# A mixture-of-experts tail: the residual rides with the first experts' rows, and three token tiles are read early

## The chip, the cores and the metric

The kernel runs on one core of one Trainium2 chip. The metric is device time in microseconds (us), the median of several executions. TensorE (PE) does the matmuls, VectorE (DVE) and ScalarE (ACT) the elementwise work, GpSimd (POOL) issues the indirect DMAs and does a few small operations, SyncE (SP) issues most of the other DMAs. All of them share the core's 16 DMA engines.

## The reference, cut to what matters

One decoder layer of 1024 tokens and width 1024. Attention comes first and is not touched. Then each token picks one of 4 expert groups and two of the group's 8 experts:

```python
x = x + gate_a * (o @ w_out)                       # residual after attention
h = rms_norm(x, g_moe) * (1 + scale_m) + shift_m
y = 0
for e in range(32):                                # gates are zero but for two experts per token
    hid = silu(h @ w_gate[e]) * (h @ w_up[e])      # 1024 -> 256
    y = y + gates[:, e:e+1] * (hid @ w_down[e])    # 256 -> 1024
x = x + gate_m * y
return rms_norm(x, g_final)
```

All arrays are float32. An expert's three matrices are 3 MB together, the 32 experts 96 MB.

## The kernel before, in words

Tokens are held as T = 8 tiles of 128 rows (XT). After the router, every (token, expert) pair is given a slot in a list of NSTEP = 20 steps of 128 slots; a step holds four pieces of 32 slots, each of one expert, the busiest experts first. What does not fit goes to an overflow list, whose loop runs only if a count that is read at run time is above zero; with these inputs it does not run.

The normed rows of all tokens lie in DRAM (h2_dram), and so does y_dram, which has 2 x 1024 rows: row t for a token's first expert and row 1024 + t for its second. The 20 steps are the expert phase:

- POOL gathers the 128 token rows of a step into SBUF (`gather`, L712). It gathers steps 0 to 3 first. Then, for each n, it issues gather(n + 4) and after it scatter(n). gather(n) waits for t_ps, that is for PE to have turned the rows of step n - 2 out of one of the two buffers xg.
- PE turns the rows (`turn_rows`, L2018), ACT and DVE scale them (`ev_t`, DVE L1545), PE multiplies with gate and up weights (`gate_up`, L2031), ACT and DVE make the hidden values (`ev_hid`, L1526 and L1528), PE turns these (L2040) and multiplies with the down weights (`down_proj`, L2054), one PSUM bank for each half of 512 columns.
- DVE multiplies each half by the modulation row out_row into one of two buffers ysb (`ev_y`, L1536), and POOL scatters the 128 rows to y_dram (`scatter`, L719).

PE's order in step n is: turn the hidden values of n, gate_up(n + 1), turn_rows(n + 2), down_proj(n). SP loads the weights into 7 + 7 places (`gate_up_load` L421, `down_load` L426): when the last step that uses a place is done on PE, SP loads the next expert there. The last loads follow the gate_up and the down_proj of step 15. After these SP reads the tokens' own rows back from h2_dram into XT (L592, tiles 0 to 5 after step 15 and the other two after step 17), since the weights had taken their place.

The tail: when all 20 scatters have landed, POOL raises rows_out (L764), and SP reads for every tile the two blocks of expert rows (L617, 16 DMAs of 512 KB). Tiles 0, 2, 4 and 6 are combined on PE (`add_into`, L2092): XT times the identity, plus each block times a diagonal of routing weights that ACT has written (L1014). Tiles 1, 3, 5 and 7 are combined on DVE by two operations (`combine`, L1579 and L1581). For each tile in the order 0 to 7 ACT takes the sum of squares (L1026), POOL makes the reciprocal root (L768, L769), DVE scales and multiplies by g_final (`finish`, L1591), and SP stores the tile (L620).

## Time and profile before

| | |
|---|---|
| median of 3 runs | 1008.46 us (1006.54 to 1008.69) |
| the profiled execution's own time | 1007.81 us |
| its span, first to last instruction | 1006.0 us |
| mean granted TensorE clock | 0.987 |
| PE busy | 953.2 us (95% of the span) |
| DVE busy | 594.4 us (59%) |
| ACT busy | 400.9 us (40%) |
| POOL busy | 119.5 us (12%) |
| bytes moved by DMA | 189.88 MB, mean 189 GB/s |

In the profile PE is TensorE's matmuls and PEld its weight loads, which overlap. A queue's engine name with a q (SPq, POOLq) is its sequencer. L712 is line 712 of the kernel before. DMA queue q1 carries what SP issues, q10 what ACT issues, q0 what POOL issues. A share of DMA of 1.00 means that all 16 DMA engines are busy. The span and the run's time differ by 1.8 us, which lies outside the instructions.

### The profile page before, as it was taken

How to read it: one execution, taken by the hardware profiler on the slowest of the kernel's cores; microseconds unless marked ns; L12 is line 12 of the kernel's file. 1: busy time of each engine (PE TensorE's matmuls, PEld its weight loads, DVE VectorE, ACT ScalarE, POOL GpSimd, SP SyncE). 2: the span in 40 equal slices, each digit the busy share in tenths (PEclk: the TensorE clock that was granted, in tenths of full speed). 3: DMA queues.
4: the chain of work that ended last, by engine and by line, in shares of the span. 5: the costliest groups of instructions: out<-in, count | busy, mean ns of one | idle time of the engine just before them, and what ended most of it. 6: DMA issues, size and time to landing. Idle time of an engine off the chain costs nothing.

```text
span 1006.0 us, 15057 instructions
## 1 busy us (share of the span) xinstructions
PE 953.2 (95%) x5352; PEld 520.0 (52%) x5352; DVE 594.4 (59%) x1597; ACT 400.9 (40%) x909; POOL 119.5 (12%) x219
## 2 busy tenths in 40 slices
PE   3899999999999999999999999999899999998984
PEld 2465576444447856677766555556533433333421
DVE  3388647999999799987777333456422222232217
ACT  6131135666660388877668221212211111121113
POOL 3001000000007510110000000000111111111004
PEclk9899999999999999999999999998999999998999
DMA  9997100110102000040000411089799999999979
GB/s 325 334 358 277 43 22 21 43 41 22 42 23 47 1 1 1 2 169 22 1 2 2 167 45 40 23 352 382 307 409 422 421 419 421 420 420 421 418 296 367
DMA packets 70381, 189.88 MB, mean 189 GB/s; under 512 B 10200, under 2 KB 37136, under 8 KB 58016
## 3 DMA queue, kind: packets, MB, share of 16 engines
q1 hardware_dynamic: 62176, 170.53, 44.2%
q0 software_dynamic: 5760, 16.78, 4.3%
q10 hardware_dynamic: 2368, 1.57, 0.6%
q8 instruction: 44, 0.72, 0.3%
q14 instruction: 33, 0.27, 0.1%
HBM read 174.17 MB, written 18.89 MB: 192 GB/s over the span
## 4 chain that ended last, share of the span: by engine, by line
PE 65%; DVE 20%; DMA 6%; issue 4%; SPq 2%; ACT 1%; POOL 1%; POOLq 0%; DVEq 0%; ACTq 0%
PE PS L2031 12%; PE PS L1908 11%; DVE BIAS L1168 8%; PE PS L2054 6%; PE PS L1801 6%; PE PS L1844 5%; PE PS L1866 4%; DMA X<-in_w_down_dram 3%; PE PS L1762 3%; PE PS L1714 3%; PE PS L1861 2%; DVE X L1232 2%; PE PS L1739 2%; PE PS L1679 2%; PE PS L2018 2%
## 5 line engine op out<-in xcount | busy, mean ns | idle before, releaser
L1714 PE MATMUL PS<-HT,X 128*128 128x512 f32 x384 | 168.8, 593 | 0.0
L1714 PEld LDWEIGHTS PS<-HT,X 128*128 128x128 f32 x384 | 72.5, 190 | 92.4 <-issue 92.4
L878 ACT ACTIVATE X<-X,nmx 128x128 f32<-128x128 f32 (+7 forms) x128 | 98.4, 770 | 51.5 <-DVE nmx L1232 51.0
L2031 PE MATMUL PS<-QKV,HT 128*32 128x512 f32 (+2 forms) x560 | 113.0, 594 | 2.4 <-ACT HT L976 1.7
L1908 PE MATMUL PS<-QKV,HT 128*128 128x512 f32 x256 | 113.7, 597 | 0.0
L1168 DVE TENSOR_SCALAR_CACHE_REDUCE BIAS<-SC,W 128x384 f32<-128x384 f32 (+3 forms) x128 | 96.4, 809 | 1.1
L1526 DVE TENSOR_TENSOR HT<-PS,HT 128x256 f32<-128x256 f32 x20 | 8.5, 425 | 140.9 <-ACT HT L984 140.9
L861 ACT ACTIVATE X<-SC,W 128x896 f32<-128x896 f32 x64 | 69.6, 1088 | 43.0 <-DVE W L1156 43.0
L1801 PE MATMUL PS<-QKV 64*128 64x512 f32 (+3 forms) x384 | 79.0, 517 | 1.6 <-DVE nmx L1232 1.1
L1908 PEld LDWEIGHTS PS<-QKV,HT 128*128 128x128 f32 x256 | 47.4, 190 | 53.7 <-issue 53.6
L1844 PE MATMUL PS<-ident,X 128*128 128x128 f32 x432 | 63.2, 279 | 2.1 <-DVE X L1250 2.0
L2054 PE MATMUL PS<-QKV,HT 128*32 128x512 f32 (+2 forms) x272 | 57.4, 630 | 4.3 <-DMA X<-in_w_down_dram 3.9
L984 ACT ACTIVATE HT<-PS 128x256 f32<-128x256 f32 x20 | 7.7, 384 | 131.8 <-PE PS L2031 131.8
L1232 DVE CUSTOM_DVE_ANT_0 X<-PS,R 128x128 f32<-128x128 f32 (+7 forms) x80 | 50.8, 673 | 14.6 <-PE PS L1801 8.6
L2031 PEld LDWEIGHTS PS<-QKV,HT 128*32 128x32 f32 (+2 forms) x560 | 32.3, 117 | 47.9 <-issue 44.2
L1844 PEld LDWEIGHTS PS<-ident,X 128*128 128x128 f32 x432 | 47.2, 141 | 11.3 <-issue 8.5
L1232 DVE CUSTOM_DVE_ANT_0 X<-PS,SC 128x1024 f32<-128x1024 f32 (+5 forms) x48 | 42.0, 887 | 17.9 <-PE PS L1801 17.8
L2031 PE MATMUL PS<-W,HT 128*32 128x512 f32 (+2 forms) x144 | 49.3, 593 | 0.0
L1536 DVE TENSOR_TENSOR HT<-PS,R 128x512 f32<-128x512 f32 x40 | 27.7, 692 | 35.0 <-PE PS L2054 34.9
L1801 PEld LDWEIGHTS PS<-QKV 64*128 64x128 f32 x384 | 31.6, 185 | 27.8 <-issue 20.4
L1060 DVE SCALAR_TENSOR_TENSOR QKV<-QKV,cact 128x512 f32<-128x512 f32 x56 | 42.1, 752 | 2.0
L1861 PEld LDWEIGHTS PS<-QKV,HT 128*128 128x128 f32 x288 | 34.5, 191 | 16.6 <-issue 9.2
(306 smaller groups left out, 1544.9 us busy)
## 6 DMA issues: line engine op xcount, KB each, us to landing
QKV<-in_w_down_dram SPq DMA_DIRECT2D x20, 1024.0 KB, 24.5
QKV<-in_w_gate_dram SPq DMA_DIRECT2D x19, 1024.0 KB, 17.3
QKV<-in_w_up_dram SPq DMA_DIRECT2D x19, 1024.0 KB, 20.4
QKV<-in_w_ada_dram SPq DMA_DIRECT2D x8, 2048.0 KB, 12.5
QKV<-in_w_ada_dram SPq DMA_DIRECT2D x8, 1024.0 KB, 12.4
X<-in_w_in_dram SPq DMA_DIRECT2D x16, 512.0 KB, 3.8
X<-in_w_down_dram SPq DMA_DIRECT2D x8, 1024.0 KB, 22.3
QKV<-expert_rows SPq DMA_DIRECT2D x16, 512.0 KB, 10.3
```

Of the source, the lines that this page charges most:

```text
L861: act.activation(RL[:, n % 2, 0:w], SC[:, sc_off[t]:sc_off[t] + w], ACT.Sign, bias=tk[:, 4, i:i + 1].bitcast(F32), scale=-1.0, accum_out=c ...
L878: act.activation(sc, sc, ACT.Exp, bias=nmx[:, i % 4, m:m + 1], scale=-1.0, accum_out=rs[:, i, m:m + 1]).then_inc(exp_done, 1)
L1060: link(dve.scalar_tensor_tensor(out=w[:, 0, :], in0=w[:, j, :], scalar=cact[:, j:j + 1], in1=w[:, 0, :], op0=ALU.mult, op1=ALU.add))
L1168: dve.tensor_scalar(BIAS[:, i % 3, 0:w], SC[:, sc_off[t]:sc_off[t] + w], thr.bitcast(F32)[:, i:i + 1], 0.0, ALU.is_lt, ALU.add, accum_out= ...
L1232: dve.tensor_tensor_reduce(sc_buf[i % 4][:, m, 0:w], PS[:, 2 * m:2 * m + 2, :].rearrange("p a n -> p (a n)")[:, BANK * n:BANK * n + w], aw ...
L1714: end = pe.matmul(PS[:, 2 * b + half, :], WS[:, b, j, :], HT[:, j, BANK * half:BANK * (half + 1)], start=(j == 0), stop=(j == KC - 1))
L1801: end = pe.matmul(PS[:, 2 * m + n + c0 // BANK, 0:c1 - c0], QKV[rows_m, q0:q0 + P], QKV[rows_m, k0 + c0:k0 + c1], start=True, stop=True)
L1844: end = pe.transpose(PS[:, 4 + g % 2, c0:c0 + P], sc_buf[i % 4][:, m, P * b:P * (b + 1)], ident[:, :])
L1861: end = pe.matmul(PS[:, 6 + h % 2, slot], turned_at(i)[:, g % 4, P * (b - b0):P * (b - b0 + 1)], vf[:, u * S + P * b:u * S + P * (b + 1)], ...
L1908: end = pe.matmul(PS[:, n % 4, :], HT[:, k, P * (n // 2):P * (n // 2 + 1)], wo[:, k, BANK * (n % 2):BANK * (n % 2 + 1)], start=(k == 0), s ...
L2031: end = pe.matmul(PS[at, 2 + b, :], hgT[b][:, P * c_ + at.start:P * c_ + at.stop], WGU[w][:, c_, :, :], start=(c_ == 0), stop=(c_ == KC - 1))
L2054: end = pe.matmul(PS[at, 5 + h, :], hidT[b][:, P * c_ + at.start:P * c_ + at.stop], WDN[w][:, c_, BANK * h:BANK * (h + 1)], start=(c_ == 0 ...
```

## The change

The residual no longer waits in SBUF or comes back from h2_dram at the end. The rows that POOL gathers for an expert are the tokens' own rows, so each step adds its result to them before the scatter: for a token's first expert the scattered row is own row + weight * out_row * y, for its second it is weight * out_row * y alone. A tile's result is then a plain sum of its two blocks.

- The rows stay in the buffers. xg and ysb give way to four buffers `held`; step n uses held[n % 4] for its gather, adds in place and scatters from there. So gather(n) for n >= 4 waits for y_out of step n - 4, that is for scatter(n - 4) to have landed, and POOL's order for each n is gather(n + 3), then scatter(n).
- `ev_y` has two dependent DVE operations for each half instead of one: PSUM = PSUM * weight * out_row, then held = held * is_first + PSUM. It no longer waits for y_out.
- The slots' weights and the flags for first experts are made ahead of step 0: `weigh_experts` moves ahead of `ev_t(0, 0)` and gets four more small operations, three operations of `spread_weights` lay the weights (each as three bfloat16 parts) out by slot, 16 bfloat16 matmuls of PE (`list_weights`, between turn_rows(0) and gate_up(0)) bring them into slot order, and DVE reduces them (`keep_weights`). SP's load of out_row and down_load(6) wait for those matmuls.
- The 8 reads back from h2_dram are gone, and so are ACT's 8 diagonals.
- Early in the kernel, ahead of the attention, two DMAs copy the first 3 tiles of x into the two halves of y_dram, so that every row holds some finite number; POOL waits for them ahead of scatter(0).
- Ahead of step LATE = 18 (when down_proj(17) is done on PE), SP waits for the scatters of steps 0 to 17 to land and reads tiles 0, 1 and 2 (6 DMAs of 512 KB). POOL waits for these reads to land before it issues scatter(18).
- After rows_out SP reads only tiles 3, 4, 5, 7, 6 (10 DMAs). POOL gathers into tiles 0, 1 and 2 those rows that steps 18, 19 and the overflow wrote (6 indirect DMAs, each of whose other indices are out of bounds and skipped). `late_rows` makes these indices on DVE during gate_up(0).
- Tiles 0, 1, 2 and 6 are summed on PE by the identity, tiles 3, 4, 5 and 7 on DVE by one addition each. The order of squares, roots and finishing is 3, 0, 4, 1, 5, 2, 7, 6.

```diff
             for n in range(NSTEP + 1):
...
-                    back = {last_use[25]: range(0, 6), last_use[26]: range(6, T)}
-                    if n - 1 in back:
-                        for t in back[n - 1]:
-                            sp.dma_start(XT[:, t, :], h2_dram[P * t:P * (t + 1), :]).then_inc(x2_back, 16)
+                    if n == LATE:
+                        for b in range(2):
+                            sp.wait_ge(y_out[b], 16 * (LATE // 2))
+                        for t in range(AHEAD):
+                            expert_rows(t, yg_ahead)
...
             def gather(n):
 
-                if n >= 2:
+                if n >= 4:
+                    pool.wait_ge(y_out[n % 2], 16 * (n // 2 - 1))
+                elif n >= 2:
                     pool.wait_ge(t_ps, n - 1)
-                pool.indirect_dma_start(out=xg[n % 2], out_offset=None, in_=h2_dram,
+                pool.indirect_dma_start(out=held[n % 4], out_offset=None, in_=h2_dram,
...
             pool.wait_ge(route_done, 2)
+            pool.wait_ge(yg_ahead, 32)
             for n in range(NSTEP):
-                if n + 4 < NSTEP:
-                    gather(n + 4)
+                if n >= 1 and n + 3 < NSTEP:
+                    gather(n + 3)
+                if n == LATE:
+                    pool.wait_ge(yg_ahead, 32 + 32 * AHEAD)
                 scatter(n)
...
             pool.sem_inc(rows_out, 1)
-            for t in range(T):
+            pool.wait_ge(route_done, 3)
+            for t in range(AHEAD):
+                for k in range(2):
+                    pool.indirect_dma_start(out=yg[t][k], out_offset=None, in_=y_dram,
+                                            in_offset=bass.IndirectOffsetOnAxis(
+                                                ap=late_row[:, EARLY * k + t:EARLY * k + t + 1], axis=0),
+                                            bounds_check=2 * S - 1, oob_is_err=False).then_inc(yg_late[t], 16)
+            for i, t in enumerate(last):
...
-            def ev_y(e, b, stored):
-
-                dve.wait_ge(y_out[b], stored * 16)
+            def ev_y(e, buf, weight, is_first, counted):
+
                 for h in range(2):
                     part = slice(BANK * h, BANK * (h + 1))
                     dve.wait_ge(dn_ps, 2 * e + h + 1)
-                    dve.tensor_tensor(ysb[b][:, part], PS[:, 5 + h, :], out_row[:, part], ALU.mult).then_inc(y_sb, 1)
+                    dve.scalar_tensor_tensor(out=PS[:, 5 + h, :], in0=PS[:, 5 + h, :], scalar=weight, in1=out_row[:, part],
+                                             op0=ALU.mult, op1=ALU.mult).then_inc(hh_done, 1)
+                    dve.wait_ge(hh_done, counted + h + 1)
+                    dve.scalar_tensor_tensor(out=held[buf][:, part], in0=held[buf][:, part], scalar=is_first,
+                                             in1=PS[:, 5 + h, :], op0=ALU.mult, op1=ALU.add).then_inc(y_sb, 1)
...
             dve.wait_ge(modc_set, 1)
+            weigh_experts()
+            link(dve.tensor_scalar(row_first[:, 0:NSTEP], PS[:, 2, NSTEP:2 * NSTEP], float(S) + 0.5, None, ALU.is_lt))
+            spread_weights(low_tok, NSTEP, weight_is)
             ev_t(0, 0)
-            weigh_experts()
...
-            pe.wait_ge(x2_back, 16 * T)
             for i, t in enumerate(mixed):
-                if i == 2:
-                    pe.wait_ge(rows_out, 1)
-                add_into(i, ident[:, :], XT[:, t, :], True, False)
-            pe.wait_ge(diag_done, 8)
-            for i, t in enumerate(mixed):
-                pe.wait_ge(yg_in[t], 32)
-                add_into(i, diag[:, i, 0, :], yg[t][0], False, False)
-                add_into(i, diag[:, i, 1, :], yg[t][1], False, True).then_inc(mix_ps, 1)
+                pe.wait_ge(yg_late[t] if t < AHEAD else yg_in[read.index(t)], 32)
+                add_into(i, ident[:, :], yg[t][0], True, False)
+                add_into(i, ident[:, :], yg[t][1], False, True).then_inc(mix_ps, 1)
```

## Rows read from the trace of the kernel before

**Rows 1.** The page: busy time of PE, and DMA's share in 40 slices.

```profile
PE 953.2 (95%) x5352; PEld 520.0 (52%) x5352; DVE 594.4 (59%) x1597; ACT 400.9 (40%) x909; POOL 119.5 (12%) x219
...
DMA  9997100110102000040000411089799999999979
```

**Rows 2.** Busy time in a stretch of five steps; last: clock, DMA share, GB/s.

```profile
800.00:860.00 60.00, 60.00 (x364) 23.23 (x362) 17.54 (x40) 11.38 (x30) 10.12 (x10) 1.00 1.02 421
```

**Rows 3.** The chain of waits in order of time: start us, length us, what.

```profile
737.29 3.57 PE PS L2054 x32
...
753.40 7.00 PE PS L2031 x64
760.41 1.09 PE PS L2018 x8
...
765.50 7.00 PE PS L2031 x64
...
785.36 3.57 PE PS L2054 x32
...
807.80 1.09 PE PS L2018 x8
...
889.43 30.68 DMA X<-in_w_down_dram
...
967.28 3.31 DMA expert_rows<-HT,SC
```

**Rows 4.** PE in order of time at its one wait for a weight.

```profile
920.36 1.08 PE L2054 MATMUL PS<-QKV,HT 128*32 128x512 f32 x3 [3.86 <-DMA X<-in_w_down_dram]
```

**Rows 5.** SP's issues in order of time: first issue us, length of the group.

```profile
929.14 22.35 SPq L592 DMA_DIRECT2D X<-h_rows  x8
970.65 9.62 SPq L617 DMA_DIRECT2D QKV<-expert_rows  x16
```

**Rows 6.** The tail in order of time: start us, length us, engine, line.

```profile
975.69 3.67 PE L2092 MATMUL PS<-QKV,SC 128*128 128x512 f32 x8 [1.31 <-DMA QKV<-expert_rows]
...
982.40 3.70 PE L2092 MATMUL PS<-QKV,SC 128*128 128x512 f32 x8 [3.04 <-DMA QKV<-expert_rows]
...
996.36 1.02 ACT L1026 ACTIVATE HT<-PS 128x1024 f32<-128x1024 f32 x1 [2.20 <-PE PS L2092]
...
1001.70 1.28 DVE L1591 SCALAR_TENSOR_TENSOR X<-X,ss,BIAS 128x1024 f32<-128x1024 f32 x1 [0.39 <-POOL ss L769]
```

**Rows 7.** DVE at the start of the expert phase; in brackets its idle time before.

```profile
717.72 1.36 DVE L1545 TENSOR_SCALAR HT<-PS,gm,modc 128x128 f32<-128x128 f32 x4 [5.62 <-PE PS L2018]
...
720.89 0.17 DVE L1492 TENSOR_SCALAR eps_row<-eps_row 128x8 f32<-128x8 f32 x1
```

**Rows 8.** The page: DVE's output operation of all steps, mean ns of one.

```profile
L1536 DVE TENSOR_TENSOR HT<-PS,R 128x512 f32<-128x512 f32 x40 | 27.7, 692 | 35.0 <-PE PS L2054 34.9
```

**Rows 9.** POOL's instructions in order of time: start us, length us, idle before.

```profile
742.44 1.02 POOL L719 DMA_INDIRECT expert_rows<-HT,SC  x1 [3.02 <-DVE HT L1536]
750.18 1.03 POOL L712 DMA_INDIRECT HT<-h_rows,SC  x1 [6.72 <-PE PS L2018]
754.53 1.01 POOL L719 DMA_INDIRECT expert_rows<-HT,SC  x1 [3.32 <-DVE HT L1536]
...
951.89 0.98 POOL L719 DMA_INDIRECT expert_rows<-HT,SC  x1 [10.21 <-DVE HT L1536]
```

**Rows 10.** Queue 0's packets, MB, DMA share, in 754:758.5 and in 758.5:763.

```profile
q0 software_dynamic: 144, 0.52, 28.5%
...
q0 software_dynamic: 144, 0.37, 20.8%
```

**Rows 11.** The view of line 712, all 20 gathers: issue to landing.

```profile
DMA to landing us min/median/max: 5.0/8.8/10.0
```

**Rows 12.** Line 421, weight loads issued at 727.1 and at 832.4: issue to landing.

```profile
DMA to landing us min/median/max: 6.0/6.0/6.0
...
DMA to landing us min/median/max: 12.7/12.7/12.7
```

More of the change, by code:

```diff
@@ L613, in _ @@
             sp.wait_ge(rows_out, 1)
-            for t in range(T):
-                for k in range(2):
-                    row = S * k + P * t
-                    sp.dma_start(yg[t][k], y_dram[row:row + P, :]).then_inc(yg_in[t], 16)
-            for t in range(T):
-                sp.wait_ge(fin_done, t + 1)
+            for i, t in enumerate(read):
+                expert_rows(t, yg_in[i])
+            for i, t in enumerate(last):
+                sp.wait_ge(fin_done, i + 1)
                 sp.dma_start(out[0, P * t:P * (t + 1), :], XT[:, t, :]).then_inc(fin_out, 16)
@@ L755, in _ @@
                 pool.wait_ge(ov_list, 2)
+                for b in range(2):
+                    pool.wait_ge(y_out[b], 16 * uses(b))
                 with pool.Fori(0, NOV // 2) as i:
@@ L1011, in _ @@
             act.dma_start(gfin, g_final.partition_broadcast(P)).then_inc(act_in, 16)
-            for i, t in enumerate(mixed):
-                for k in range(2):
-                    act.activation(diag[:, i, k, :], ident[:, :], ACT.Copy, scale=rt[:, 5 + k, t:t + 1]
-                                   ).then_inc(diag_done, 1)
-            for t in range(T):
+            for n, t in enumerate(last):
                 if t in mixed:
@@ L2061, in weights_of, with list_weights @@
                         sorted({(w % places, 16 * (w // places + 1)) for w, _, _ in parts[n]}))
-            turn_rows(0, 0, 16)
+            def list_weights(bank, at, tiles, rows, weights):
+                for q in range(T):
+                    for k in range(2):
+                        end = pe.matmul(PS[:, bank, at:at + 3 * tiles], rows[:, k, q, :],
+                                        weights[:, k, q, :, :].rearrange("p a n -> p (a n)"),
+                                        start=(q == 0 and k == 0), stop=(q == T - 1 and k == 1))
+                return end
+            turn_rows(0, 0, 16, 0)
+            pe.wait_ge(weights_at, 3)
+            list_weights(6, 0, NSTEP, row_is, weight_is).then_inc(sel_ps, 1)
             gate_up(0, 0, *weights_of(0, GUS))
-            turn_rows(1, 1, 16)
+            turn_rows(1, 1, 16, 1)
             for n in range(NSTEP):
```

159 lines of the change are left out of this document (106 added, 53 removed).

## The prediction

> **What bounds the kernel now.** I read the page first, then the chain of waits over the last 350 us, then the busy times by stretch, and last POOL's own timeline with the packets of its queue. PE is busy for 95% of the span [rows 1], and DMA's row of slices is empty in the middle and full from about 650 us on [rows 1]. In the expert phase both are full: PE 60.00 us of 60, and DMA at a share of 1.02 with 421 GB/s [rows 2]. The chain of waits runs on PE, one step in 12.1 us (gate_up starts at 753.40 and at 765.50), up to a down weight that was issued at 889.43 and lands 30.68 us later, at 920.1 [rows 3]; PE has then waited for it for 3.86 us [rows 4]. What the reader is to see: a step that becomes longer ahead of 916 us is free up to those 3.9 us in all, and dear beyond them. After the last step comes a tail: the last scatter takes 3.31 us [rows 3], reads start at 970.65 [rows 5], the last tile is finished at 1001.70 + 1.28 = 1002.98 [rows 6], and its store ends at 1006.0.
>
> **The start of the phase.** DVE is idle for 5.6 us ahead of 717.7, while the first gather is under way [rows 7]. The 10 moved operations, four new ones, one flag and the three larger ones go there: 15 small ones at 0.2 us (the 10 stood between 719.1 and 721.1 [rows 7]) are 3.0 us, three of 320 elements at no more than the 0.69 us of a 512-element one [rows 8] are 2.1 us. They end some 0.5 us ahead of 717.7. PE's 16 small matmuls lie beside ACT's and DVE's scaling of the first rows, 1.36 us on DVE [rows 7]. Cost 0; if the cover fails, 1 us at most. The load of out_row is first used 20 us later. The copies of x into y_dram lie where DMA's slices are at 0 or 1 tenths [rows 1]: 0.
>
> **DVE and ACT in the steps.** A half's output takes two dependent operations instead of one. I price the second like the first, 0.69 us [rows 8], and with the wait between them 0.75 us. DVE has 17.5 us of work in 60 [rows 2], so 3 us more per step do not make it the bound. What counts is that scatter(n) can be issued 0.75 us later. The bank is free again well before the next down_proj.
>
> **The gathers: the term that decides.** Before, gather(n + 4) waited only for PE's turning of step n + 2. Now it waits for scatter(n) to land, as its buffer is the one that is scattered. The chain from the end of down_proj(n) to landed rows of step n + 4, piece by piece:
> - down_proj(0) ends at 737.29 + 3.57 = 740.86 [rows 3], its scatter is issued at 742.44 [rows 9]: 1.58, now with 0.75 more 2.33 us.
> - Scatter issued to landed. No row gives it, as nobody waited for it visibly. Scatter(1) is issued at 754.53 [rows 9]; queue 0 moves 144 packets in 754:758.5, which are those of the gather issued at 750.18 (at the median it lands at 759.0), and 144 more in 758.5:763, which are the scatter's [rows 10]. So it takes up to 8.4 us; the bounds are 3.31, the last scatter with DMA nearly idle [rows 3], and 10.0, the slowest gather [rows 11]. I take 8.1, near to the row of the same operation under the same load.
> - The landing to POOL's next issue: 0.8 us, as from the end of turn_rows(3) at 749.4 to 750.18 [rows 9].
> - The gather: 8.8 us, bounds 5.0 and 10.0 [rows 11].
>
> The sum is 20.0 us. PE wants the rows at 760.41 [rows 3], 19.55 us after 740.86; for step 4 the distance is 807.80 - 788.93 = 18.9 [rows 3]. With a mean of 19.3 the chain is 0.7 us too long, and as it spans two of PE's steps, that alone lengthens a step by 0.35 us.
>
> But there is a second loop. Gather and scatter share queue 0. The gather's 144 packets and the scatter's 144 stand one behind the other and do not mix [rows 10], so I read it as one queue in order, though in this case the scatter came just late enough not to wait. Then the new order is: scatter(n) lands, 0.8, gather(n + 4) takes 8.8, and only behind it go the packets of scatter(n + 1), which need another 3.7 us (758.5 to 763 is 4.5 at the most, and a step's scatter moves 0.37 MB against 0.52 of that gather [rows 10]). One round of the loop is 0.8 + 8.8 + 3.7 = 13.3 us, against 12.1 for PE's step: 1.2 us more per step, as soon as scatter(n + 1) waits behind gather(n + 4), which is so from step 1 (the gather comes at 743.19 + 8.1 + 0.8 = 752.1 and lands at 760.9, the scatter at 755.3 would have its packets move from 759.3).
>
> The Trainium skill (DMA: Bandwidth & Descriptors, Queues, rings and completion order) says that each DMA engine takes the descriptors of one ring in order and switches between rings by the packet. By that rule gathers and scatters queue up as in my second loop, and the weights of SP's queue are interleaved with both.
>
> How many steps are stretched? Steps 4 to 19 give 15 intervals. The weights' backlog is what stretches the latencies, and it is least near 832 us: a load takes 12.7 us there against 6.0 when the queue had just begun to fill [rows 12], so it holds 6.7 us of work. PE's lateness of 1.2 us per step uses that up after some six steps; then DMA has gaps, gather and scatter fall towards 5.0 and 3.3 us, the loop is 12 us or less and nothing is added for about four steps. That leaves 11 intervals: 11 x 1.2 = 13.2, and the first stall 0.6 (760.9 + 0.1 against 760.41), in sum 13.8 us. Of that 3.9 us disappear in the wait at 916 us [rows 4], as the weights' arrival is set by DMA, which stays busy: **+9.9 us** at the last down_proj. Its ends: 0 (the latencies of a quieter queue) and 15 x 1.5 + 0.6 - 3.9 = 19.
>
> **The tail.** The 8 reads back (from 929.14 on, 4 MB [rows 5]) came after the last weights, so dropping them makes no weight earlier; they only leave DMA idle for the early reads. Scatter(17) is landed some 4 us after its issue with DMA quiet. Then SP reads 3 tiles. Before, with as empty a queue, tile 2 was there at 982.40 - 970.65 = 11.7 us after the first issue [rows 5, 6]. Scatter(18) waits for this: from scatter(17)'s issue 4 + 0.4 + 11.7 + 0.8, then 1.3 for the next issue and 3.3 for scatter(19) to land, 21.5 us. Before, from its issue at 951.89 [rows 9] to 970.65, it was 18.8; with DVE's 0.75 the reads of the tail start **3.5 us later** relative to PE (ends 1 and 6).
>
> After that start, called R, POOL's first two gathers of the late rows are issued at R + 0.7 and R + 2.0, and land by R + 7 to R + 9 (5.0 to 8.8 us, few rows); PE's four sums of 3.7 us each [rows 6] run from about R + 7.5 to R + 22.3, and tile 6 is there by R + 18. The last sum ends at 996.3; the tile's square, root and finishing are over by 1001.7, when the next is finished [rows 6]: 5.4 us, say 5.0; then 3.0 for the store (1002.98 to 1006.0). End at R + 30.3, against 1006.0 - 970.65 = 35.35 before [rows 5, 6]: **-5.0 us** (ends -8 if DVE and POOL keep closer, -2 if stores and reads collide). Late next is then PE's row of four sums.
>
> **Sum**, against the profiled execution's 1007.81: + 0 (start) + 9.9 (gathers) + 3.5 (scatter(18) held back) - 5.0 (fewer reads in the tail) = +8.4, so 1016.2. The profiled execution lies 0.65 below the median of 1008.46, within the runs' own spread of 2.2; I do not correct for it and say 1016.
>
> **The rivals.**
> - *A, the forecast:* queue 0 is in order and the loop of 13.3 us rules. For it: two kinds of row, [rows 11] and [rows 10], and the saturated DMA of [rows 2]. Against it: the scatter's 8.1 is inferred. 1016, own range 1011 to 1023. Chance 0.5.
> - *B, no queueing between gather and scatter, only the 20.0 us against 19.3:* 15 x 0.35 = 5.3, less 3.9 hidden, +1.4; with the tail's -1.5, no change: 1007.7. Chance 0.17.
> - *C, the other side: the chain fits in.* One mechanism: gather plus scatter under load take 0.7 us less than I say, 16.2 instead of 16.9, and the queueing stays below the slack; from 19.3 us down PE never waits. For it: some gathers land in 8.1 us, and DVE's 0.75 may be partly hidden. Then only the tail counts: +3.5 - 5.0 = -1.5, and with the better ends of both (+1, -5) down to -4: 1003.8 to 1006.3, likeliest 1005.5. Chance 0.17.
> - *D, the early reads give nothing:* A's steps, and scatter(18) is held for the full 6 us while the tail keeps its length but for 2: +9.9 + 6 - 2 = 1021.7. Chance 0.09.
> - *E, the loop never finds a quiet stretch:* 19 - 1.5 = +17.5 and more, 1025 to 1030. Chance 0.07.
>
> The Trainium skill has a rule by which C would win outright (the same page, Anatomy of one DMA): an indirect or other DMA of POOL takes about 2.0 us plus its bytes over 436 GB/s, an estimate of 3.0 us for 0.42 MB. The sum would be 2.33 + 3.0 + 0.8 + 3.0 = 9 us, far below 19, and the time 1006.3. The trace agrees only where DMA is quiet (3.31 us for the last scatter) and not in the steps (8.8 us), so this adds nothing to C's chance.
>
> **How the numbers follow.** About 0.2%, 2 us, is what a measurement can tell from no change. Slower: A, D and E, 0.66, less the part of A's low end that is below +2 (0.04): 0.62. Faster: most of C, 0.14. The same: B and the rest, 0.24. The range leaves out E's upper part and C's lowest part: 1005 to 1024.
>
> **What would show it.** In the profile of the changed kernel, waits of PE at turn_rows for the gather: some 14 us in about ten waits, steps of 13.3 us, and the wait for a down weight near 916 us gone or small. Scatters' packets that begin more than 4.0 us after their issue. SP's wait ahead of the early reads 4 to 5 us, POOL's wait ahead of scatter(18) some 8 us. The tail from SP's first late read to the end about 30 us. The forecast is wrong if PE never waits for a gather: then it is C.

## The result, and the profile after

| | before | after |
|---|---|---|
| median of the runs made side by side | 1008.23 us (4) | 1020.23 us (4; 1018.30 to 1022.01) |
| ratio, 95% interval | 1 | 1.0122, 1.0099 to 1.0145 |
| profiled execution | 1007.81 us | 1018.3 us |
| span of that execution | 1006.0 us | 1016.5 us |

The change makes the kernel slower by 12.0 us, and by 10.5 us between the two profiled executions, which is the difference that the views below account for. (The profiled execution of after is the fastest of its four.) The forecast was +8.4, in the range.

The page of after, against [rows 1] of before: PE's busy time and DMA's slices.

```profile
PE 946.7 (93%) x5352; PEld 518.8 (51%) x5352; DVE 626.0 (62%) x1645; ACT 398.1 (39%) x901; POOL 122.6 (12%) x225
...
PEclk9999999999999999999999999997999999999978
DMA  9997101011015000040000411299899989999577
```

DVE has 32 us more, nearly all of it the second operation of 40 halves at 0.75 us. PE has 6.5 us less work in a span that is 10.5 us longer, so it waits more. The row of clocks hides what matters below: the falls of the clock in the steps are too short for a slice of 25 us.

Busy times by stretch of after, columns as in [rows 2]; last are the granted clock, DMA's share and GB/s.

```profile
740.00:780.00 40.00, 37.35 (x316) 13.25 (x309) 15.61 (x31) 6.81 (x18) 6.22 (x7) 1.00 1.01 420
780.00:820.00 40.00, 36.33 (x166) 15.51 (x168) 15.69 (x30) 6.81 (x18) 6.67 (x7) 1.00 1.01 415
820.00:860.00 40.00, 37.96 (x237) 14.23 (x230) 15.50 (x30) 6.81 (x18) 6.21 (x7) 0.96 0.90 366
900.00:940.00 40.00, 37.13 (x248) 13.98 (x248) 15.67 (x30) 6.81 (x18) 6.07 (x6) 1.00 1.01 420
```

PE was busy for all of 800:860 before. Now it lacks 2 to 4 us of every 40. DMA stays full except in 820:860, where its share falls to 0.90: the quiet spell that the forecast speaks of. It is short: the share is 0.34 in 820:825, 0.80 in 825:830 and 1.01 from there on.

The waits of after: engine, line, what was waited for; us in total, times, the longest. L739 is the gather, L746 the scatter, L2093 PE's turning of the gathered rows, L2180 PE's sums of the tail, L617 SP's wait ahead of the early reads.

```profile
POOL HT L739 <- DMA expert_rows<-HT,SC: 133.2, 15, 10.2
...
PE PS L2180 <- DMA QKV<-expert_rows,SC: 17.9, 1, 17.9
...
PE PS L2093 <- DMA HT<-h_rows,SC: 15.1, 11, 2.2
...
POOL expert_rows L746 <- DMA SC<-expert_rows: 13.3, 1, 13.3
```

POOL now waits for a scatter to land before each of its 16 gathers from gather(4) on (one of these waits, of 10.4 us, the view puts down to "issue"), and PE waits 11 times, 15.1 us in all, for gathered rows. Before it waited for none of more than 0.4 us in sum. The wait for a down weight [rows 4] is gone.

The chain of waits of after, in order of time, against [rows 3]: start us, length us, what.

```profile
741.22 10.06 DMA expert_rows<-HT,SC
...
752.06 8.09 DMA HT<-h_rows,SC
...
760.19 1.16 PE PS L2093 x8
761.35 3.62 PE PS L2129 x32
...
764.99 0.77 DVE PS L1596
...
765.78 0.76 DVE HT L1599
...
767.33 9.06 DMA expert_rows<-HT,SC
...
777.15 9.29 DMA HT<-h_rows,SC
...
786.48 1.16 PE PS L2093 x8
```

Before, this chain ran on PE alone. Now it goes round: scatter, gather, turn, down_proj, DVE's two operations, scatter, and one round takes 786.48 - 760.19 = 26.3 us for two of PE's steps.

The same round in POOL's own order, against [rows 9].

```profile
752.06 1.03 POOL L739 DMA_INDIRECT HT<-h_rows,SC  x1 [9.81 <-DMA expert_rows<-HT,SC]
753.39 1.02 POOL L746 DMA_INDIRECT expert_rows<-HT,SC  x1 [0.30 <-issue]
764.21 1.01 POOL L739 DMA_INDIRECT HT<-h_rows,SC  x1 [9.80 <-DMA expert_rows<-HT,SC]
```

Scatter(1) is issued at 753.39, 1.3 us behind a gather, and has landed 0.8 us before 764.21: 10.0 us, where I had priced 8.1.

### The profile page after: what moved, and what is told of

It reads as the page before. It is cut to its first block, busy times and chain, and to the rows that moved or that the text cites. A ratio compares the mean times of both kernels' runs of the same rounds, so it can differ in the third digit from the quotient of the medians.

```text
span 1016.5 us, 15086 instructions
## 1 busy us (share of the span) xinstructions
PE 946.7 (93%) x5352; PEld 518.8 (51%) x5352; DVE 626.0 (62%) x1645; ACT 398.1 (39%) x901; POOL 122.6 (12%) x225
## 4 chain that ended last, share of the span: by engine, by line
PE 55%; DVE 20%; DMA 16%; issue 6%; ACT 1%; POOL 1%; SPq 0%; POOLq 0%; DVEq 0%; ACTq 0%
PE PS L1983 11%; DVE BIAS L1205 8%; DMA expert_rows<-HT,SC 7%; DMA HT<-h_rows,SC 6%; PE PS L1876 6%; PE PS L1919 5%; PE PS L2129 4%; PE PS L1941 4%; PE PS L2106 3%; PE PS L1837 3%; PE PS L1789 3%; PE PS L1936 2%; DVE X L1269 2%; PE PS L1814 2%; PE PS L2180 2%
## 5 line engine op out<-in xcount | busy, mean ns | idle before, releaser
L1919 PEld LDWEIGHTS PS<-ident,X 128*128 128x128 f32 x432 | 47.2, 141 | 11.4 <-issue 8.7
L1269 DVE CUSTOM_DVE_ANT_0 X<-PS,SC 128x1024 f32<-128x1024 f32 (+5 forms) x48 | 42.0, 887 | 17.9 <-PE PS L1876 17.8
L1876 PEld LDWEIGHTS PS<-QKV 64*128 64x128 f32 x384 | 31.6, 185 | 27.8 <-issue 20.4
L1017 ACT ACTIVATE HT<-PS,modc,gm 128x128 f32<-128x128 f32 x80 | 30.1, 455 | 36.4 <-PE PS L2093 36.4
## 6 DMA issues: line engine op xcount, KB each, us to landing
QKV<-in_w_ada_dram SPq DMA_DIRECT2D x8, 2048.0 KB, 15.6
```

The source lines that it names most:

```text
L1269: dve.tensor_tensor_reduce(sc_buf[i % 4][:, m, 0:w], PS[:, 2 * m:2 * m + 2, :].rearrange("p a n -> p (a n)")[:, BANK * n:BANK * n + w], aw ...
L1876: end = pe.matmul(PS[:, 2 * m + n + c0 // BANK, 0:c1 - c0], QKV[rows_m, q0:q0 + P], QKV[rows_m, k0 + c0:k0 + c1], start=True, stop=True)
L1919: end = pe.transpose(PS[:, 4 + g % 2, c0:c0 + P], sc_buf[i % 4][:, m, P * b:P * (b + 1)], ident[:, :])
```

## Where the 10.5 us went

POOL's issue times cut each profile into stretches that can be compared. G0 is the first gather's issue, S0, S17 and S19 those of scatters 0, 17 and 19, end is the end of the span. All times in us; the last column is what PE waited for on gathers and weights from G0 to S17. Waits for gathers of 0.3 to 0.7 us lie ahead of S0.

| kernel | G0 to S0 | S0 to S17 | S17 to S19 | S19 to end | PE's waits |
|---|---|---|---|---|---|
| before | 31.35 | 209.45 | 15.39 | 38.72 | gathers 0.4, a down weight 3.9 |
| after | 31.87 | 221.88 | 15.62 | 37.78 | gathers 15.1 in 11 |
| e1_wait_alone | 31.96 | 219.42 | 15.37 | 39.76 | gathers 15.7 in 15 |
| e2_light_weights | 31.87 | 214.56 | 17.07 | 37.11 | gathers 10.2 in 6 |
| e3_five_buffers | 32.26 | 213.95 | 16.38 | 36.93 | gathers 10.5 in 10 |
| e4_own_result_buffer | 32.68 | 207.96 | 22.37 | 36.45 | gathers 0.5, a weight 2.4 |
| e5_second_op_alone | 32.22 | 207.50 | 15.40 | 39.10 | gathers 0.5, a weight 3.3 |
| e6_late_rows_behind | 31.88 | 209.33 | 16.02 | 39.52 | a weight 3.7 |
| e7_two_ahead | 32.03 | 206.86 | 14.05 | 39.28 | a weight 3.2 |
| e8_quiet_weights | 32.82 | 202.32 | 16.92 | 36.78 | gathers 0.7 |
| e9_clock_kept | 32.13 | 208.67 | 13.85 | 46.19 | a weight 3.1 |
| e10_sums_sooner | 32.58 | 208.54 | 14.06 | 42.15 | gathers 0.5, a weight 2.8 |
| e11_clock_kept_short | 32.64 | 205.84 | 14.85 | 35.27 | gathers 0.5, a weight 1.9 |
| e12_plan_alone | 32.38 | 207.70 | 13.85 | 36.34 | gathers 0.3, a weight 2.1 |

Of after less before: +0.5 up to S0, **+12.4 in the steps**, +0.2 and -0.9 in the tail, and -1.7 ahead of G0 (709.35 against 711.09; in the executions of all these kernels it lies between 708.4 and 712.1 without order, so it is not the change's). The sum is 10.5.

The steps need one more look, at the one wait of before. The chain of before has the weight wait, and down_proj behind it:

```profile
920.11 0.25 issue
920.36 6.47 PE PS L2054 x32
```

and the stretches of before around it, columns as above (the last but two is the granted clock):

```profile
916.00:918.00 2.00, 0.50 (x5) 0.30 (x3) 1.91 (x6) 1.49 (x5) 0.73 (x1) 1.00 1.01 422
918.00:920.00 2.00, 0.00 (x0) 0.00 (x0) 0.22 (x1) 0.04 (x1) 0.28 (x1) 0.82 1.01 426
920.00:922.00 2.00, 1.64 (x8) 0.46 (x12) 0.00 (x0) 0.00 (x0) 0.00 (x0) 0.50 1.01 418
922.00:924.00 2.00, 2.00 (x16) 0.67 (x12) 0.00 (x0) 0.00 (x0) 0.00 (x0) 0.50 1.00 410
...
926.00:928.00 2.00, 2.00 (x18) 0.60 (x14) 0.69 (x1) 0.38 (x1) 0.00 (x0) 0.97 0.98 406
```

While PE stands still for 3.86 us its granted clock falls to 0.50, the 1.2 GHz level, and stays there for some 6 us of the work behind: this down_proj takes 6.47 us where others take 3.57 [rows 3]. So the wait cost 3.86 + 2.90 = 6.8 us, not 3.9, and before's 17 steps without it are 202.7 us, 11.9 each. After's are 221.88 / 17 = 13.05 each: 19.2 us added by the round, and 6.8 taken off with the weight wait that it hides.

The same happens once more in after. Two of its eleven waits, of 2.04 and 2.18 us, are followed by a lower clock; the chain of after at the first:

```profile
850.41 1.85 PE PS L2093 x8
852.26 4.54 PE PS L2129 x16
```

and the stretches there:

```profile
848.00:850.00 2.00, 0.37 (x4) 0.00 (x0) 0.85 (x2) 0.38 (x1) 0.00 (x0) 1.00 1.03 416
850.00:852.00 2.00, 1.59 (x8) 1.45 (x8) 0.00 (x0) 0.00 (x0) 0.00 (x0) 0.67 0.99 412
852.00:854.00 2.00, 2.00 (x8) 0.58 (x8) 1.37 (x4) 1.50 (x4) 0.00 (x0) 0.50 1.04 438
```

Turning and down_proj take 6.39 us where they take 1.16 + 3.62 = 4.78 in the other steps: 1.6 us more, and 1.3 at the second (1.97 + 4.14). The two steps are the longest of after, 15.8 and 15.7 us from scatter to scatter. With them the 19.2 us are 15.1 of waits, 2.9 of clock and 1.2 left over (behind a wait, turning takes 1.16 in place of 1.09 us). A wait of 2.24 us at 760.19 left the clock at 1.00, and so did one of 3.15 us for the same down weight in e7 below, so the length of the wait alone does not decide it.

## The experiments

The theory after the result: the scatter that must land before a gather is issued makes a round of DMA latencies, and these are long because weights fill DMA. Rivals: DVE's second operation costs the time; the order in queue 0 does, and not the chain through PE; the early reads and the tail do.

**e1: the wait alone.** The kernel before, with nothing but the gather's wait and its place in POOL's order.

```diff
             def gather(n):
+                if n >= 4:
+                    pool.wait_ge(y_out[n % 2], 16 * (n // 2 - 1))
...
-                if n + 4 < NSTEP:
-                    gather(n + 4)
+                if n >= 1 and n + 3 < NSTEP:
+                    gather(n + 3)
```

> The kernel before with one part of the change alone: gather(n + 4) also waits for scatter(n) to have landed (nothing else needs it here), and POOL issues gather(n + 3) ahead of scatter(n). One DVE operation for each half, residual and tail as before. Loop theory (PE waits for gathers that wait for landed scatters while DMA is saturated): slower than before, by one of two sizes. If only the chain down_proj, scatter, gather, turn_rows counts: 1.6 + 9.0 + 0.7 + 9.3 = 20.6 us against 19.3, over two steps, 0.6 us per step, 15 steps, less the 3.9 us hidden at the weight: +5, about 1013 us. If also the order in queue 0 counts (scatter behind gather, a round of 13.1 us): 1.0 us per step, +11, about 1019 us. Rival (the second DVE operation, the extra work at the start or the tail made it slower): within 1 us of before, 1008.

Measured: 1018.98 us against 1006.61, 1.0131 (1.0100 to 1.0163). The chain of waits of e1 (L2020 turns the rows, L2056 is down_proj):

```profile
795.19 9.48 DMA expert_rows<-HT,SC
...
805.49 8.47 DMA HT<-h_rows,SC
...
814.00 1.16 PE PS L2020 x8
```

The wait, with its place in POOL's order, is the whole loss. The kernel has no second operation on DVE, no early read, the old tail, and is as slow as the changed kernel; its steps take 219.4 us, 2.5 less than after's, and the clock does not fall in them (1.00 in all five stretches of 40 us), which is 2.9 of after's. The time is that of the larger of the two sizes expected, the one with the order in queue 0 in it; what that order adds here is read in the account of the prediction below.

**e5: DVE's second operation alone.** The kernel before, with two dependent operations for a half (the second adds 0.0 times a row, so that the result is the same).

```diff
-                    dve.tensor_tensor(ysb[b][:, part], PS[:, 5 + h, :], out_row[:, part], ALU.mult).then_inc(y_sb, 1)
+                    dve.tensor_tensor(PS[:, 5 + h, :], PS[:, 5 + h, :], out_row[:, part], ALU.mult).then_inc(hh_done, 1)
+                    dve.wait_ge(hh_done, counted + h + 1)
+                    dve.scalar_tensor_tensor(out=ysb[b][:, part], in0=out_row[:, part], scalar=0.0, in1=PS[:, 5 + h, :],
+                                             op0=ALU.mult, op1=ALU.add).then_inc(y_sb, 1)
```

> The kernel before with one other part of the change alone: DVE makes each half of a step's result in two dependent operations (the second adds the PSUM half to a row times zero). Gathers as before. Loop theory: nothing waits for DVE here, the last scatter is issued 0.8 us later; 0 to +1 us against before. Rival (the second operation stretches the steps): +0.9 us per step, up to +12 us.

Measured: 1006.79 against 1006.09, 0.9996 (0.9979 to 1.0014): no change. The later scatter costs nothing as long as nobody waits for it to land.

**e8: light weights.** The changed kernel, with the later weight loads cut to 256 of 2048 columns.

```diff
-                        gate_up_load(sp, expert_of(w), w % GUS)
+                        gate_up_load(sp, expert_of(w), w % GUS, n=256)
...
-                        down_load(sp, expert_of(w), w % DNS)
+                        down_load(sp, expert_of(w), w % DNS, n=256)
```

> The changed kernel, with all instructions of PE, DVE, ACT and POOL, but the weight loads from place 7 on bring only 256 of 2048 columns each (a part of the computation left out), as the loads of half size had left DMA busy at 0.8 to 0.9. Loop theory: DMA's share in the steps below 0.5, scatters and gathers land in 5 to 6 us, no wait of PE for a gather, steps of 12.1 us: from the first to the eighteenth scatter 206 to 208 us instead of 222, about 1002 to 1005 us in all. Rival (second DVE operation, PSUM written back by DVE): steps stay at 13 us.

Measured: 1000.09 against 1006.09, 0.9932 (0.9908 to 0.9957), 2 us under what was expected, as the landings and the steps are shorter than I had said. A stretch of e8, and the landing of its 20 scatters and 20 gathers:

```profile
740.00:780.00 40.00, 40.00 (x328) 14.37 (x321) 16.34 (x32) 7.02 (x19) 7.12 (x7) 1.00 0.40 129
```

```profile
DMA to landing us min/median/max: 2.9/3.4/4.3
...
DMA to landing us min/median/max: 3.6/4.3/10.2
```

and the same two views of after:

```profile
DMA to landing us min/median/max: 3.3/9.2/10.4
...
DMA to landing us min/median/max: 4.4/8.7/10.4
```

With DMA's share at 0.27 to 0.40 in the stretches of the steps a scatter lands in 3.4 us in place of 9.2 and a gather in 4.3 in place of 8.7, and PE waits for none in the steps. The wait is the same, the two transfers of the round are 10 us shorter together. That is what ties the loss to the weights' traffic and not to the wait as such. S0 to S17 is 202.32 us, which is what before's steps take without their weight wait (202.7): the 6.8 us priced above, from another side.

The Trainium skill (DMA: Bandwidth & Descriptors, Latency and other measured facts) puts the access of HBM at 0.2 us on average and 2 us at high load. The trace agrees in the direction only; the difference between e8 and after is 4.4 us for a gather and 5.8 for a scatter.

The traces' packet records show where it lies. A packet of 4 KB of queue 0 takes 0.159 us in e8 and in after alike (median of 740 to 940 us), so the packets do not become slower. They begin later and stand further apart. In after the first packet of scatter(0) comes 4.1 us after its issue, at 745.34, though queue 0 had sent nothing before it; in e8 it is 1.6 us. From a scatter's first to its last packet it is 3.3 to 5.3 us in after's steps under full DMA, and 1.0 to 2.3 us in e8, where the weights' packets are about as many but take 0.046 us each in place of 0.309. Ahead of that first packet DMA moves weights alone; behind gather(4)'s issue at 752.06, the view of queues in 752.5:756 has no queue but SP's:

```profile
q1 hardware_dynamic: 198, 1.47, 99.9%
```

What holds the first packet back for 2.5 us more than in e8, no run here shows.

**e2: half the gate and up weights.** The same as e8 with 1024 of 2048 columns and full down weights.

> The changed kernel, but from expert place 7 on each gate and each up load brings only half of its columns (0.5 MB instead of 1 MB); the other half of the place keeps old values, so that part of the computation is left out. PE, DVE, ACT and POOL do the same instructions. Loop theory: with DMA at about 0.7 of its share, scatters land in some 5 us and gathers in some 6 us, the chain is 14 us against 19.3, PE waits for no gather, and the wait for a down weight is gone too: 12.5 and some us less than the changed kernel, about 1004 to 1007 us, steps of 12.1 us. Rival (DVE's second operation or an extra PE instruction stretches the steps): steps stay at 13 us, 1016 us or more.

Measured: 1014.41 against 1006.61, 1.0090 (1.0053 to 1.0127). A miss: I had expected 1004 to 1007. The stretch 860:900 of e2 shows why:

```profile
860.00:900.00 40.00, 35.80 (x256) 13.70 (x258) 15.58 (x30) 6.57 (x18) 6.10 (x6) 0.96 0.93 324
```

DMA moved 324 GB/s, a quarter less, and was still busy for 0.93 of the time. The down weights, gathers and scatters were as large as ever, and of the halved rows' packets (4 KB in place of 8) half took no more than 0.159 us, against 0.309 for a full one, but their mean in this stretch was 0.197. So this run did not take the load away, and e8 had to.

**e3: a fifth buffer.** The changed kernel, with the gather waiting for the scatter of a step earlier, into one buffer more; for each n POOL issues gather(n + 4), then scatter(n), and g_final is loaded after the last scatter.

```diff
-        held = [HF[:, a:a + 1024] for a in (0, 1024, 4096, 5120)]
+        held = [BIAS[:, 2, :]] + [HF[:, a:a + 1024] for a in (0, 1024, 4096, 5120)]
...
-                if n >= 4:
-                    pool.wait_ge(y_out[n % 2], 16 * (n // 2 - 1))
+                if n >= 5:
+                    pool.wait_ge(y_out[(n - 5) % 2], 16 * ((n - 5) // 2 + 1))
```

> The changed kernel with a fifth row buffer (in the third kilobyte row of BIAS; g_final, which comes to lie there, is loaded after the last scatter): gather(n + 4) waits for scatter(n - 1) instead of scatter(n), everything else the same. Loop theory: PE gets 12 us more slack per gather, its waits for gathers are gone or small, steps of 12.1 us, total about 1008 us (start 0, tail -0 to -2 against before). If the order in queue 0 makes a loop of its own (round of 13.1 us), POOL falls behind PE by some 1 us per step: scatters issued to landed and gathers drift later through the phase, and the last few gathers may make PE wait a few us, 1008 to 1012. Rival (DVE's second operation, start, tail): 1018 or more, as the changed kernel.

Measured: 1012.04 against 1006.61, 1.0061 (1.0044 to 1.0078). Half of the loss is back, and what is left is the other round of the forecast. POOL's order in e3:

```profile
767.30 1.02 POOL L739 DMA_INDIRECT HT<-h_rows,SC  x1 [11.47 <-DMA expert_rows<-HT,SC]
768.62 1.02 POOL L746 DMA_INDIRECT expert_rows<-HT,SC  x1 [0.30 <-issue]
781.33 1.02 POOL L739 DMA_INDIRECT HT<-h_rows,SC  x1 [11.68 <-DMA expert_rows<-HT,SC]
782.65 1.01 POOL L746 DMA_INDIRECT expert_rows<-HT,SC  x1 [0.30 <-issue]
```

A gather, 1.3 us later a scatter that has long been ready, and 11.9 us later it has landed, which lets the next gather go. The chain of waits of e3 runs from scatter to scatter, with PE in none of its pieces:

```profile
782.65 10.63 DMA expert_rows<-HT,SC
...
795.42 11.22 DMA expert_rows<-HT,SC
```

Six of these in a row take 10.4 to 11.9 us, 11.2 on average, 2 us more than the 9.1 of the scatters in after's chain. The steps from scatter to scatter are 12.5 to 14.0 us, 13.3 on average, up to the sixteenth. This is the forecast's round through queue 0, at its size of 13.3 us. The packet records agree: the packets of these scatters begin 6.0 to 6.9 us after their issue (scatters 1 to 14), when the gather's are through, and not 4.1 to 4.3 us after it as with the queue free.

**e4: an own buffer for the result.** DVE writes the output to a buffer of its own, so the gather needs only DVE, and no landed scatter. POOL issues scatter(n) first and gather(n + 4) behind it, and DVE's output of a step waits for the scatter of the step before to have landed.

```diff
-                if n >= 4:
-                    pool.wait_ge(y_out[n % 2], 16 * (n // 2 - 1))
+                if n >= 4:
+                    pool.wait_ge(y_sb, 2 * (n - 4) + 2)
...
-                    dve.scalar_tensor_tensor(out=held[buf][:, part], in0=held[buf][:, part], scalar=is_first,
+                    dve.scalar_tensor_tensor(out=ysb[:, part], in0=held[buf][:, part], scalar=is_first,
```

> The changed kernel, but DVE writes the step's result into a buffer of its own (the same kilobyte row of BIAS) and POOL scatters from there. gather(n + 4) then waits only for DVE to have read the rows of step n, no longer for a scatter to land; POOL issues scatter(n), then gather(n + 4); DVE's result of step n + 1 waits for scatter(n) to have landed. Loop theory: the chain is 2.4 + 1.3 + 9 to 11 = 13 to 15 us against 19.3, PE waits for no gather, 12.1 us per step, about 1007 to 1009 us. No drift, as no gather hangs on a landed scatter. Rival (second DVE operation or tail): 1018 or more.

Measured: 1010.99 against 1006.61, 1.0041 (1.0020 to 1.0061), 2 us over what was expected. The steps are back to 207.96 us, with 0.5 us of waits for gathers. But S17 to S19 went from 15.6 to 22.4 us: the one result buffer makes step 19's output wait for scatter(18), which itself waits for the early reads.

**e6 and e7: that wait removed, and the tail in another order.** In e6 step 19 writes in place, and the tiles with late rows are summed last; e7 is e6 with two tiles read early in place of three, and the order of the tail's tiles fitted to that.

```diff
-                in_=ysb, in_offset=None,
+                in_=held[n % 4] if n == NSTEP - 1 else ysb, in_offset=None,
...
-        AHEAD = 3
-        read = (3, 4, 5, 7, 6)
+        AHEAD = 2
+        read = (2, 3, 4, 6, 5, 7)
```

> The kernel with a result buffer of its own, with two edits. Step 19 adds in place and is scattered from its row buffer, so it no longer waits for scatter(18). In the tail PE sums tile 3, which is read directly, first and then 0, 1, 2; DVE sums 4, 5, 7, 6; squares and finishing go in the order 3, 4, 5, 0, 7, 6, 1, 2. Loop theory with the tail as the late gathers' and PE's sums set it: the last scatter 5 us earlier than with the result buffer alone, the last sum of PE ends some 22 us after the tail's first read instead of 26: 6 to 9 us less than that kernel, 2 to 4 us less than before. If the tail is bound by the bytes it moves, only the 5 us of the scatter are won, and the time is that of before.

> The same with only two tiles read early instead of three: the early reads take some 4 us less, so that scatter(18) is no longer held by them for long, and one more tile (1 MB, 2.6 us) is read after the last scatter. If the hold counts, the last scatter is issued 1 to 1.5 us earlier and the whole is within 1.5 us of the kernel with three; if the tail's bytes count, it is 1 to 2.5 us slower.

Measured: e6 1008.12 and e7 1005.40 against 1006.09, 1.0016 (0.9999 to 1.0032) and 0.9990 (0.9977 to 1.0004). Both are level with before. The result buffer's wait is gone (S17 to S19 is 16.0 and 14.1 us), but both are misses: e6 was to be 2 to 4 us under before, and e7 within 1.5 us of e6 or slower, where its median is 2.7 us lower. With the round gone the early reads bring nothing that can be measured in these. PE has nothing to do between its last down_proj and the first rows of the tail, and the first sum then takes 6.56 us (e6) and 5.30 us (e7) in place of 3.7 [rows 6]; whether that is what the time goes by, the next four test.

**e9 to e12: PE kept at work, and DVE's order.** e9 is e7 with 48 multiplies into an unused bank ahead of the sums; e10 the same with the tiles' sums and finishing steps on DVE in another order; e11 is e10 with 26 multiplies; e12 is e10 without any.

```diff
+            for _ in range(48):
+                pe.matmul(PS[:, 7, 0:2 * P], ident[:, :], HT[:, KC - 1, BANK:BANK + 2 * P], start=True, stop=True)
             for i, t in enumerate(mixed):
```

```diff
             combine(3)
-            finish(2)
             combine(4)
+            finish(2)
...
             finish(0)
+            combine(7)
             finish(6)
             finish(1)
-            combine(7)
             finish(7)
```

> The kernel with a result buffer of its own and two tiles read early, plus 48 matmuls of 256 columns on PE between the last down_proj and the first sum of the tail, into a PSUM bank that nobody reads; they fill the 12 us in which PE was idle and the granted clock fell to 0.50, so that the first sum took 5.3 us. If that clock is on the chain: the first sum takes 3.7 us and the whole is 1 to 2 us less. If DVE's order of work or the bytes bound the tail: no change, within 0.5 us.

> The same with the 48 matmuls, and DVE adds tile 4 ahead of finishing tile 2, and tile 7 ahead of finishing 6 and 1 (before, it added tile 7 some 5 us after its rows had landed, and the last two tiles waited for that). If DVE's order is the tail's bound: 3 to 5 us less than with two tiles early alone, about 1001 us, 4 to 6 us less than before. If the tail is bound by the bytes of reads and stores: at most 1 us less.

> e10_sums_sooner with 26 idle multiplies in place of 48. In e10 they took 20.99 us for 96 records (0.437 us a call) and held the first sum back to 9.6 us behind the landing of its rows; 26 take 11.4 us, which ends them at about 973.8 us where e7_two_ahead's rows landed at 973.7. If the clock is what lengthened e7's first sum: the sum is at 3.5 to 3.7 us (5.3 in e7), the granted clock in 966:974 is near 1.00, and from the end of the first sum to the end it is 18.9 us as in e10 (22.5 in e7): span near 997, median 1000 to 1002, 0.7% under before. If the tail goes by the arrival of the last rows, it is within 1 us of e12.

> e7_two_ahead with only VectorE's order of sums and finishing steps in the tail changed, and no idle multiplies. If VectorE's order is what e10 gained over e9 (18.9 against 22.5 us behind the first sum), this is 1 to 3.5 us under e7_two_ahead: 1002 to 1004.4. If the last rows' landing is what ends the tail, it is e7's time (1005.4). The first sum stays at 5.3 us, at the fallen clock; e11 less this run is what the clock is worth, 1.6 us or less.

Measured: e9 1011.24 and e10 1009.45 against 1007.01, 1.0043 (1.0026 to 1.0061) and 1.0021 (1.0008 to 1.0034); e11 1003.03 and e12 1002.04 against 1005.55, 0.9975 (0.9958 to 0.9993) and 0.9964 (0.9945 to 0.9982). e9 and e10 miss because of their own size: the 48 multiplies took 20.99 us, two records a call, and held up the first sum. e11 has the size right. PE's sums and the multiplies ahead of them in e11, in order of time:

```profile
963.43 13.18 PE L2199 MATMUL PS<-HT,ident 128*128 128x256 f32 x52 [2.18 <-issue]
976.45 3.60 PE L2194 MATMUL PS<-SC,ident 128*128 128x512 f32 x8
```

and the first sum in e12, without multiplies:

```profile
976.60 5.78 PE L2194 MATMUL PS<-SC,ident 128*128 128x512 f32 x8 [13.82 <-DMA SC<-expert_rows]
```

The clock had fallen in e11 too (0.76 in 962:966, 0.81 in 966:970), but with the multiplies it is back at 1.00 in 970:974, where it is 0.50 in e12, and the first sum is 2.2 us shorter with it. So work on PE does bring the clock back and keep it. It does not pay, though: e11 is 1.0 us above e12 in the median, with intervals that overlap. In e11 the rows of a tile that DVE needs land only at 982.05 (its chain of waits), and PE's gain ends in a wait for them. DVE's order probably pays: e12 less its kernel before is -3.5 us, where e7's is -0.7, and e10 less e9, the same two orders with the multiplies, is -1.8 us; in both pairs the intervals just overlap. Against the forecast of 1002 to 1004.4 it is right, and e11's 1000 to 1002 is missed by 1.0.

**The version to keep** of all these is e12: 0.9964 of before, -3.5 us. It is the changed kernel with the result in a buffer of its own (so that no gather waits for a landed scatter), two tiles early, and DVE's order of e10. The gain is small, 0.18 to 0.55%.

## Why the prediction was right, and where its sizes were off

- *The start: 0.* G0 to S0 is 31.87 against 31.35, of which DVE's second operation is 0.75 by the forecast. Right.
- *DVE's second operation: +0.75.* From the end of down_proj(17) at 960.73 to scatter(17) at 963.10 is 2.37 us, forecast 2.33, and 1.55 before. Right, and e5 shows that it is free by itself.
- *The chain, 20.0 us.* The seven rounds in the chain of waits of after have 2.4 us from the end of down_proj to the scatter's issue (forecast 2.33), a scatter of 9.1 (8.50 to 10.06; forecast 8.1), 0.8 (0.8) and a gather of 9.2 (8.09 to 9.67; forecast 8.8): 21.5 us. The scatter is what I mis-sized. I had taken its price from one row of queue 0 whose packets ended by 763 [rows 10].
- *Which round rules: the step that failed.* The forecast let the queue's round (13.3) rule and gave the chain 0.35 us a step. The chain of waits of after runs through the chain: (21.5 + 4.8) / 2 = 13.1 us a step, with 4.8 for turning and down_proj. Its seven rounds cover 14 of the 17 steps; the other three go at PE's own pace (11.4 to 12.5 us from down_proj to down_proj), and with the two falls of the clock the mean is 13.05. It is B's chain with a scatter 1 us longer and a gather 0.4 us longer than priced, and it comes out at nearly A's size. Queueing behind a gather isn't needed for that: scatter(0), issued after POOL had sent nothing for 14 us, is the slowest of the chain with 10.06 us.
- *A's queue is real all the same.* By the packet records (queue 0 moves 144 packets for a gather or a scatter; I count them off in order of time) a scatter's packets in after begin 4.1 to 4.3 us after its issue where DMA is full and the gather was issued 3.5 us or more ahead of it. Where under the same load it was issued 1.3 to 3.1 us ahead, they begin 4.7 to 6.0 us after it, which is always 7.4 to 8.2 us after the gather's issue, so behind the gather's packets. In after this hardly touches the chain: its four scatters that stood behind a gather took 9.0 us on average, its three others 9.3. In e1, where DVE has one operation and the scatter follows the gather by some 2 us in most steps, the scatters of the chain took 10.2 us, and that uses up what the shorter DVE work saves. In e3, where the fifth buffer gives the chain room, A's round rules alone, with its 13.3 us. So for the changed kernel a forecast with only the chain in it and the right latencies would have been as good, and A's number was right in part by luck.
- *A sign that could not tell.* "Packets that begin more than 4.0 us after their issue" was to show the queue. In the trace of before, where every gather was issued 3.8 us or more ahead of the scatter, the scatters' packets already begin 4.1 to 4.5 us after their issue.
- *The steps, +9.9.* Measured +12.4. The term of 11 intervals at 1.2 and 0.6 (13.8) was 19.2: 17 intervals at 1.13. The quiet spell came close to where it was said (820:830, with a share of 0.34 at first; the forecast named 832 as the weakest point), but it was short: gather(9) and scatter(6) were quick (6.1 and 4.8 us), and PE went two steps without a wait, where four had been forecast; PE's waits were 15.1 us in 11, forecast 14 in about ten. Left out were the falls of the clock, 2.9. The hidden weight wait was 6.8 and not 3.9, as its length on PE is not its cost. The two errors, +5.4 and -2.9, took part of each other away.
- *Scatter(18) held back, +3.5.* From S17 to SP's first late read, R = 983.47, it is 20.4 us against 18.8, so +1.6. The hold itself costs nearly nothing. down_proj(19) ends at 976.09, its scatter could be issued 2.4 us later at 978.5, and it was issued at 978.72. Scatter(18), ready at about 974.1 (971.75 + 2.4), waited until 977.45, but scatter(19) was what the late reads needed. The early reads had landed at 976.68, 10.1 us behind SP's first issue (forecast 11.7). What did cost is the last scatter, 4.69 us in place of 3.31 [rows 3], right behind scatter(18).
- *The tail from R, 30.3.* It is 1016.5 - 983.47 = 33.0, against 35.35 before: -2.3 and not -5.0. The chain of waits of after shows the piece that failed:

```profile
978.72 4.69 DMA expert_rows<-HT,SC
...
985.64 8.27 DMA QKV<-expert_rows,SC
...
993.95 15.74 PE PS L2180 x32
1009.72 1.02 ACT HT L1063
```

  PE's first sum began at R + 10.5 and not at R + 7.5. The gather of the late rows was priced for few rows; it shared DMA with ten reads of SP (share 0.97 to 1.03 in 986:994) and took 8.3 us. Then the sums took 15.7 for 14.8 us at a clock of 0.50 at first, after PE had stood for 17.9 us. The rest was 6.8 for 8.0.
- *The sum.* In the forecast's terms 0 + 9.9 + 3.5 - 5.0; measured 0.5 + 12.4 + 1.6 - 2.3 and -1.7 ahead of G0, which is 10.5. Each sign was right, the largest term was a fifth too small.
- *The rivals.* B's chain came true and its size did not; its premise that nothing queues did not hold in e1 and e3, nor for after's scatters off the chain. C, the other side, needed gather and scatter to take 16.2 us or less; they took 18.3. The Trainium skill's rule by which C would have won (DMA: Bandwidth & Descriptors, Anatomy of one DMA) gives some 6 us for the two, an estimate; the trace comes near it only where DMA is quiet: in e8, with DMA at a share of 0.27 to 0.40, they took 7.7. D and E did not come: the tail did become shorter, and the quiet spell did come.

## What to carry to other kernels

Before a buffer is shared between a read and the write that frees it, add up the round (issue, landing of the write, issue, landing of the read) with latencies from rows at the load of that very stretch, and count what stands ahead of each transfer in its queue: here 3.4 and 4.3 us became 9.2 and 8.7. If two transfers share a queue, look also at how far apart they are issued: behind a gather issued 2 us ahead, a scatter took 10.2 us and not 9.1. Price a wait of TensorE by the time to the next undisturbed step, with the slower work behind it, and not by its length; that holds for waits that a change removes as well. Reads taken out of a tail are worth only what the next engine in it, here VectorE's order of sums, can use.

## What was not expected of the hardware

- The granted clock fell from 1.00 to 0.50 in waits of 3.86 us (before), 2.04 and 2.18 us (after) and stayed at 1.00 through waits of 2.24 us (after), 2.11 us (e1) and 3.15 us (e7). Work at 0.50 took up to 1.8 times as long: 6.47 for 3.57 us.
- 26 small multiplies in a gap of 13 us brought it back from 0.50 to 1.00 (e11: 0.76 in 962:966, 1.00 in 970:974; e12 without them: 0.50 in 970:974), and the sum behind took 3.60 us in place of 5.78 (e12).
- With gate and up rows of half the length DMA was busy for 0.78 to 0.93 of the time at 287 to 327 GB/s (e2), where full rows give 1.02 at 421 [rows 2].
- A scatter's long landing under load is not slower packets (0.159 us for 4 KB in e8 and in after) but a later first packet (4.1 us after the issue in place of 1.6) and more time between them. What delays the first packet stays open.
